# Two transformer blocks on one core: side work moved by some steps in the second block's projections

## The reference

```python
q, kv, gates, gq, gk, gv, glr, gout = split(rms_norm(h, attn_norm) @ w_in)
kc, vc, ks, vs, kw, vw = split(kv)              # 2 groups of 64 each
q = partial_rope(rms_norm(q, q_gain), pos) * scale
# compressed branch: windows of 32 tokens, stride 16, 31 of them
k_cmp = partial_rope(rms_norm(gelu((kc[blk] + pe_k) @ w1_k) @ w2_k, k_gains[0]), end)
v_cmp = gelu((vc[blk] + pe_v) @ w1_v) @ w2_v
o_cmp = masked_softmax(q @ k_cmp.T) @ v_cmp
# selected and window branches: keys ks and kw, normed and rotated, causal at 512 tokens
o_nsa = g0 * o_cmp + g1 * attend(q, ks, vs) + g2 * attend(q, kw, vw)
# gated linear attention, decays from glr
log_a = log_sigmoid(glr @ w_gate2 + b_gate) / 16
h = h + concat([o_nsa, gla(gq, gk, gv, log_a, gout)]) @ w_out
```

## Time and profile before

| | us |
|---|---|
| three runs | 1628.07, 1628.36, 1631.10 |
| median | 1628.36 |
| profiled execution, its own time | 1628.07 |
| its span | 1626.3 |

### The profile page before, as it was taken

One profiled execution on the slowest core, in us unless ns is written; L12 is line 12 of the kernel. 1 busy time (PEld: TensorE's weight loads), 2 busy tenths in 40 slices (PEclk: granted clock), 3 DMA queues, 4 the chain that ended last, 5 costly groups with the idle time before them and its releaser, 6 DMA issues.

```text
span 1626.3 us, 19784 instructions
## 1 busy us (share of the span) xinstructions
PE 1590.8 (98%) x8003; PEld 1268.0 (78%) x8003; DVE 881.5 (54%) x1628; ACT 614.2 (38%) x1069; POOL 43.8 (3%) x82
## 2 busy tenths in 40 slices
PE   6999999999999999999999999899999999999999
PEld 5877877678888888888888886666768888887887
DVE  6769785655375653232333655676457455555432
ACT  4443334542312432222322454466425334344320
POOL 1000000000000000000000101100000000000000
PEclk8999999999999999999999999999999999999999
DMA  7512121136245334322222151110113222222221
GB/s 299 198 65 103 53 75 69 53 129 246 104 168 168 104 131 155 104 91 101 86 99 99 34 188 47 39 53 14 40 53 116 91 104 91 88 85 100 104 78 52
DMA packets 44883, 165.76 MB, mean 102 GB/s; under 512 B 5108, under 2 KB 5236, under 8 KB 43640
## 3 DMA queue, kind: packets, MB, share of 16 engines
q1 hardware_dynamic: 44792, 164.50, 28.8%
HBM read 162.38 MB, written 2.10 MB: 101 GB/s over the span
## 4 chain that ended last, share of the span: by engine, by line
PE 91%; DVE 4%; ACT 2%; issue 1%; POOL 1%; DMA 0%; SPq 0%; DVEq 0%; ACTq 0%
PE bank L526 87%; PE bank L535 4%; DVE AR L1656 1%; DVE AR L1663 1%; DMA X<-in_x 0%; DVE wl L1644 0%; POOL ST L2420 0%; DVE X L1656 0%; ACT wh L1150 0%; ACT AR L1161 0%; ACT AR L1173 0%; DVE CST L1656 0%; POOL ST L2418 0%; DVE ST L1666 0%; DVE Hl L1656 0%
## 5 line engine op out<-in xcount | busy, mean ns | idle before, releaser
L526 PE MATMUL bank<-wh,Hh 128*128 128x512 f32 (+1 forms) x1008 | 408.8, 406 | 0.4 <-DVE wl L1644 0.4
L526 PE MATMUL bank<-wh,Hl 128*128 128x512 f32 (+1 forms) x1008 | 392.6, 390 | 0.0
L526 PE MATMUL bank<-wl,Hh 128*128 128x512 f32 (+1 forms) x1008 | 392.2, 389 | 0.0
L1150 ACT ACTIVATE wh<-raw 128x1024 fp32r<-128x1024 f32 (+2 forms) x195 | 203.6, 1047 | 403.6 <-PE bank L526 391.4
L1644 DVE TENSOR_TENSOR wl<-raw,wh 128x1024 fp32r<-128x1024 f32 (+2 forms) x195 | 234.3, 1209 | 138.9 <-ACT wh L1150 138.3
L526 PEld LDWEIGHTS bank<-wh,Hh 128*128 128x128 f32 x1008 | 190.5, 189 | 58.0 <-issue 21.7
L526 PEld LDWEIGHTS bank<-wh,Hl 128*128 128x128 f32 x1008 | 190.2, 189 | 40.5
L526 PEld LDWEIGHTS bank<-wl,Hh 128*128 128x128 f32 x1008 | 190.7, 189 | 34.3
L526 PE MATMUL bank<-Hh,wh 128*128 128x512 f32 (+2 forms) x504 | 190.5, 378 | 2.6 <-DVE AR L1663 1.2
L526 PE MATMUL bank<-Hh,wl 128*128 128x512 f32 (+2 forms) x504 | 189.4, 376 | 0.0
L526 PE MATMUL bank<-Hl,wh 128*128 128x512 f32 (+2 forms) x504 | 189.3, 376 | 0.0
(11 more groups left out here) (245 smaller groups left out, 1878.5 us busy)
## 6 DMA issues: line engine op xcount, KB each, us to landing
raw<-in_wst SPq DMA_DIRECT2D x268, 512.0 KB, 3.6
AR<-in_wst SPq DMA_DIRECT2D x8, 1024.0 KB, 6.5
X<-in_x SPq DMA_DIRECT2D x8, 512.0 KB, 4.9
AR<-in_wst SPq DMA_DIRECT2D x5, 512.0 KB, 6.0
out<-X SPq DMA_DIRECT2D x8, 256.0 KB, 2.1
CST<-in_cst SPq DMA_DIRECT2D x1, 1619.0 KB, 9.6
raw<-in_wst SPq DMA_DIRECT2D x4, 296.0 KB, 2.8
BC<-in_bc SPq DMA_DIRECT2D x2, 512.0 KB, 6.9
```

The costliest lines, as they stand in the source:

```text
L526: return e.matmul(o, l, r, start=start, stop=stop, skip_group_check=True)
L1150: e.activation(HI[slot[i]][:, 0:width(i)], raw[:, i % NR, 0:width(i)], ACT.Copy).then_inc(*w_hi.mark(i))
```

## The change

It moves side work between steps on TensorE, ScalarE and VectorE. No arithmetic changes. In terms of steps:

| work | before | now |
|---|---|---|
| `scale` of ks on VectorE | 2kw step 8 | 2kw step 4 |
| transposes and copies of ks | 2kw step 14 | 2kw step 12 |
| `comp` chunks 2 and 3 | 2nq steps 2 to 9 | 2nq steps 4 to 11 |
| transposes and copies of kw | 2nq step 9 | 2nq step 12 |
| first decay sum and its exponentials | 2nq step 12 | 2nq step 11 |
| gelu on ScalarE | 2nq step 10 | 2nq step 12 |
| gelu's transposes | 2nq step 11 | 2nq step 13 |
| `ck`, `cv` | 2nq step 13, bank 6 | 2nq step 14, banks 4 and 5 |
| transpose `kc` | 2gv step 2 | 2gv step 1 |
| first attention unit | 2gv step 2 | 2gv step 1 |
| `cscore` of the first query tile | 2gv step 4 | 2gv step 2 |
| from `cscore` to `pct` | 3 steps | 2 steps |
| from one `cscore` to the next | 4 steps | 3 steps |

The core of the diff (of several like edits one stands):

```diff
@@ TensorE
-                    w.after(15, lambda: turn_keys("ks"))
+                    w.after(13, lambda: turn_keys("ks"))
...
-                    w.after(10, lambda: turn_keys("kw"))
+                    w.after(13, lambda: turn_keys("kw"))
...
                         if q == 3:
                             x.then_inc(*small.mark(("comp", c)))
                         yield
+                    if c == 1:
+                        yield
+                        yield
...
                 yield
-                yield
                 on.wait_ge(*dve.of(("hid",)))
-                claim(6)
+                claim(4)
                 for k in (0, 1):
-                    x = mm(bank[6][0:64, 256:320], hid4[:, k, 0, :], ...
+                    x = mm(bank[4][0:64, 0:64], hid4[:, k, 0, :], ...
                 x.then_inc(*small.mark(("ck",)))
+                free[4] = dve.of(("ck", "read"))
+                claim(5)
...
-                            x = mm(bank[6][32 * r4:32 * r4 + 32, 64 * g:64 * g + 64], ...
+                            x = mm(bank[5][32 * r4:32 * r4 + 32, 64 * g:64 * g + 64], ...
                 x.then_inc(*small.mark(("cv",)))
-                free[6] = dve.of(("ck", "read"))
-                for _ in range(5):
-                    yield
+                free[5] = dve.of(("vc",))
+                yield
+                yield
+                yield
...
                     yield
                     yield
-                    yield
                     on.wait_ge(*dve.of(("cprob", i)))
...
             def second_attention():
-                yield
                 yield from attention(att2, ...
@@ ScalarE
-                w.after(15 if name == "ks" else 10, lambda: [out_(u) for u in (0, 1)])
+                w.after(13, lambda: [out_(u) for u in (0, 1)])
...
-                for _ in range(25):
+                for _ in range(27):
                     yield
                 on.wait_ge(*small.of(("comp", 3)))
                 e.activation(hidr, bank[7][:, 0:256], ACT.Gelu_apprx_tanh)...
@@ VectorE
-                w.after(9 if name == "ks" else 5, scale)
+                w.after(5, scale)
...
-                for _ in range(27):
+                for _ in range(28):
                     yield
                 on.wait_ge(*small.of(("hid",)))
```

More of the change, by code:

```diff
@@ L960, in compressed @@
                 yield
-                yield
                 on.wait_ge(*dve.of(("hid",)))
-                claim(6)
+                claim(4)
                 for k in (0, 1):
-                    x = mm(bank[6][0:64, 256:320], hid4[:, k, 0, :], W("w2k").rearrange("p (k d) -> p k d", k=2)[:, k, :], k == 0, k == 1)
+                    x = mm(bank[4][0:64, 0:64], hid4[:, k, 0, :], W("w2k").rearrange("p (k d) -> p k d", k=2)[:, k, :], k == 0, k == 1)
                 x.then_inc(*small.mark(("ck",)))
+                free[4] = dve.of(("ck", "read"))
+                claim(5)
                 for r4 in range(4):
@@ L969, in compressed @@
                         for k in (0, 1):
-                            x = mm(bank[6][32 * r4:32 * r4 + 32, 64 * g:64 * g + 64], hid4[:, k, 1, 32 * g:32 * g + 32],
+                            x = mm(bank[5][32 * r4:32 * r4 + 32, 64 * g:64 * g + 64], hid4[:, k, 1, 32 * g:32 * g + 32],
                                    W("w2v").rearrange("p (k d) -> p k d", k=2)[:, k, :], k == 0, k == 1)
                 x.then_inc(*small.mark(("cv",)))
-                free[6] = dve.of(("ck", "read"))
-                for _ in range(5):
-                    yield
+                free[5] = dve.of(("vc",))
+                yield
+                yield
+                yield
                 on.wait_ge(*dve.of(("ck", "two")))
@@ L1017, in decays @@
                     yield
-                for _ in range(3):
-                    yield
+                yield
+                yield
                 for t in range(T):
@@ L1488, in compressed @@
                 e.activation(hidr, bank[7][:, 0:256], ACT.Gelu_apprx_tanh).then_inc(*act.mark(("gelu",)))
-                for _ in range(11):
-                    yield
+                yield
+                yield
+                yield
+                yield
+                yield
+                yield
                 for i in range(T):
@@ L2182, in compressed @@
                     q4 = slice(32 * r4, 32 * r4 + 32)
-                    copy(vc[q4, :, r4, :], bank[6][q4, 0:P].rearrange("p (g d) -> p g d", g=2), *[("vc",)] * (r4 == 3))
+                    copy(vc[q4, :, r4, :], bank[5][q4, 0:P].rearrange("p (g d) -> p g d", g=2), *[("vc",)] * (r4 == 3))
                 n3 = TK[0:64, 0:64].rearrange("p (g d) -> p g d", g=1)
                 sq = TK[0:64, 128:192].rearrange("p (g d) -> p g d", g=1)
-                src, ss = bank[6][0:64, 256:320].rearrange("p (g d) -> p g d", g=1), ST[0:64, 60:61]
+                src, ss = bank[4][0:64, 0:64].rearrange("p (g d) -> p g d", g=1), ST[0:64, 60:61]
                 on.wait_ge(*small.of(("ck",)))
```

8 lines of the change are left out of this document (removed).

## The result

| | before | changed |
|---|---|---|
| runs | 4 | 4 |
| median, us | 1628.47 | 1640.52 |
| lowest to highest | 1628.07 to 1631.10 | 1638.69 to 1641.33 |
| span of the profiled execution | 1626.3 | 1638.6 |
| mean granted clock | 0.994 | 0.991 |

A forecast was written before the change was run, and what follows sets the result against it. TensorE, 98% busy, bounds the kernel through its pauses and clock. Pauses +4.3 and clock -0.6 gave +3.7 to +3.9; +3.9 was taken on 1628.07: 1632.0 us, 8-in-10 range 1627.0 to 1635.0.

The forecast's parts named there:

- about 10 us: TensorE's waits between 930 and 1250 us in the old trace, 0.6% of the span, bounding what removed pauses could win.
- A: Start of the compression matmuls, near 963: keys' scaling ahead of the last additions, a 4.5 us pause, 4.1 us more.
- B: Gelu, 1000 to 1018: the old wait of 3.05 goes, new waits sum to 3.65, so +0.6 us.
- C: Compressed keys and first scores, 1021 to 1038: waits of 4.35 against the old 4.25, +0.1 us.
- the three later ones: Three later TensorE waits of 0.3 to 0.4 us on VectorE's addition, one per further query tile, expected to stay.
- the fourth queries' scaling 2.25 and the probabilities stand together ahead of the transposes: 1.6: In C, TensorE waits 1.6 us for VectorE's scaling and probabilities (1.7) before the transposes, with 2.4 of TensorE work between.
- Clock: Low-clock term: -2.9 us for two old stretches, +1.5 at A, +0.8 for one stretch in B or C, together -0.6.
- Rival 3: Slower than forecast: the clock falls at A, in B and in C, +5.9 us, 1634.0; chance 0.12.
- Rival 1: Only A's cost is left, C's pause before the probabilities is covered, clock full behind A: 1628.7 to 1631.0; chance 0.28.
- rival 2: Faster: B and C lose their waits altogether and the low clock goes, against 5.6 at A: -4.6 us, 1623.5; chance 0.13.
- Rival 4: Each table switch on ScalarE also pays a drain, so B's two switches cost 2.8 us more: 1634.8; chance 0.03.
- The leading step taken out of the attention: Attention ends one step earlier, but the linear attention after it starts in the same step as before: gain nothing.

The follow-up runs named there:

- a_alone: The kernel before with only the keys' scaling after 5 steps instead of 9 and their turn after 13 instead of 15: 1634.76 us, ratio 1.0034.
- turn_early: The changed kernel with the turns and copies of the third and fourth queries' tiles one step earlier: 1636.30 us, ratio 1.0044 to the kernel before.
- fill_all: The changed kernel with idle matmuls, results not read, in six TensorE pauses and no wait removed: 1632.62 us, ratio 1.0022 to the kernel before.
- gelu_late: The kernel before with TensorE's transposes of the gelu's result two steps later and the decay sums one step later: 1625.17 us, ratio 0.9968.
- best: gelu_late with the gelu's transposes in bank 3 and the fourth queries' tile scaled one step later: 1618.84 us, ratio 0.9940 to the kernel before.
- combo: The changed kernel with undo_a, turn_early and bank6 together: 1628.99 us, ratio 0.9998 to the kernel before.
- undo_a: The changed kernel with the keys' scaling behind the last additions again and their turn after 15 steps: 1632.16 us, ratio 1.0021 to the kernel before.
- bank6: The changed kernel with ck and cv in bank 6 again instead of banks 4 and 5: 1634.75 us, ratio 1.0038 to the kernel before.
- fill: The changed kernel with idle matmuls in two pauses, before the compression and before the first probabilities' transposes: 1636.27 us, ratio 1.0036 to the kernel before.

## Why the prediction was wrong

- **What bounds the kernel**: right. Every edit changed the time through TensorE's pauses and clock, as the sum over twelve traces shows. The rows given for "about 10 us" add up to 8.9; the rest is a wait of 1.46 near 1220 that the change does not touch.
- **A**: right. Forecast a pause of 4.5 and 4.1 us more, measured 4.47 and 4.07; a_alone shows it by itself. The clock behind it was sized at 1.5 (bounds 0.6 and 3.1); 4.6 us of work at the low level are 0.46 x 4.6 = 2.1.
- **B**: the waits forecast were 0.35, 0.1, 1.6 and 1.6; measured are 0.34, 1.03, 1.69 and 1.58. The gelu's was missed. Two copies of the window keys, one of the queries and a weight tile stand ahead of its table load, which begins at 1010.84, while TensorE is there at 1011.55. The length of ScalarE's chain was right (5.25 forecast; 5.3 from 1009.23 to the end of the second decay's second exponential), but the sum left out the weight tile ahead of it (1008.28 to 1009.23). The decay sum's 1.69 hangs on the same chain: the two waits together are 2.72 against 1.7, so that 1.69 lies near 1.6 is partly luck. B came to 4.64 against 3.65.
- **C**: forecast 1.0, 0.75, 1.6 and, for the rest, 1.0; measured 1.15, 0.67, 3.62 and nothing, together 5.44 against 4.35. (The wait of 0.28 at 1049.73 is one of the three later ones, which stayed as forecast.) The step that failed is "the fourth queries' scaling 2.25 and the probabilities stand together ahead of the transposes: 1.6". It asks only when the operand is ready; that wait would have been 1.15, to the probabilities' end, so it was not too small. The bank that the transposes write was not looked at, and it came free 2.3 us later. turn_early took the sharing away and the pause went with it, though there the low clock ahead of the place had part in it. The trace of before already had such a wait: the third tile's turn, whose operand VectorE had finished by 1024.3, stood 1.77 us until VectorE had copied the compressed keys out of bank 2 (1030.12).

```profile
1030.40 0.66 PE L535 MATMUL bank<-CST,AR 128*128 128x128 f32 x4 [1.77 <-DVE PRMT L1669]
```

- **Clock**: the term "-2.9 for the two old stretches, +1.5 at A, +0.8 for one stretch in B or C", -0.6 in all, is the step of the sum that failed most. Measured: +6.6 us. The loss for each us of low work was right (0.47 forecast, 0.46 fitted). What was wrong is how much work fell under it: in B 3.4 us (1.6) and in C 13.3 us (6.1), where half a stretch had been put for both. Rival 3 had the right shape, the clock falls in A, B and C, but gave each place one stretch. That the stretches need the pauses, and that the small matmuls alone don't bring them, was shown by fill_all: full clock with all small matmuls in place and the pauses filled.
- **Sum**: pauses +6.8 against +4.3, clock +6.6 against -0.6. Of what the forecast lacked, 7.2 us are clock and 2.5 are pauses, of these 1.0 in B, 1.1 in C and the 0.5 that it took off for longer product steps, which no trace shows; 1.2 of it is missing in the span, since the first compression wait begins 1.2 us earlier in this execution than in that of before. The range ended at 1635.0 because it held one more stretch and no longer one.
- **Rival 1 and 2** (only A is left, or faster) are out: B and C together are 10.1 us of pauses, and 3 was the point below which rival 2 would have come. What they took for possible is real, though: gelu_late and best win at these same two places, with other moves.
- **Rival 4** (a drain at each table switch) is out. The table load at 1010.84 starts 0.02 after the copy before it ends, and the gelu 0.02 after the load, so there is no room for a drain. The Trainium skill (ScalarE: Activation LUTs, What ACT_TABLE_LOAD costs) adds a drain of some 1.4 us to each; neither kernel shows it.
- **The leading step taken out of the attention** was not tried by itself; in combo it stands and costs nothing that can be seen.

Not settled: why the clock stayed low through 13.3 us of nearly unbroken work behind the pause of 3.62, when it rose after 4.6 us of work behind the pause of 4.47 and after 3.4 behind B. Two traces show it alike, and with shorter pauses in C (undo_a, bank6) no such long stretch follows. Nor is it settled when the clock falls. With the same pauses of 1.58, 1.15 and 0.67 one after the other it fell within 1 us of the end of the last of them in undo_a, turn_early and fill, and in neither trace of the changed kernel. So the order of the work sets the pauses, but not by itself the low stretches, and how much of a single edit's gain is clock could not have been foretold from its pauses. What decides either, no run tells apart.

## What to carry to other kernels

When work is moved towards its reader, ask for each waiting instruction two times: when its operand is ready, and when the buffer that it writes is free; the second can hang on a third engine's queue. Where one engine is 98% busy, count its pauses twice, once as they stand and once for the clock: here each us of TensorE's work behind a standstill that runs at the low level costs 0.46 us more, and that came to as much as the pauses themselves. Here the cheap win was not to bring the producer forward but to let the waiting reader come later, behind product steps that were ready anyway.

## What the runs showed of the hardware

- Idle matmuls hold the clock: 53 of them in six pauses kept it at the full level for 99 us and took 7.9 us off the time. The Trainium skill (TensorE: Matmul & The Clock Gate, The HAM clock gate) says that "the default state is throttled, and activity releases the throttle". The runs agree in this: with the pauses filled the level stayed full, and behind A it rose after 4.6 us of work. Behind C it rose only after 13.3 us of work, which I had not expected.
- At the low clock a kernel's own waits get shorter (bank 2: 3.62 in the changed kernel, 2.18 in undo_a and 1.15 in bank6, all with the same order there). The other engines keep their speed: VectorE's 128x512 product takes 0.68 at 1039.43 in turn_early's low stretch and 0.69 at 1035.47 in the changed kernel at the full clock. A pause read from one trace is worth its length only while the clock ahead of it stays as it is.
- In the first 30 us of the program the low clock lasts 0, 7, 10 or 14 us in different executions, with no difference in the order there. It does not explain the spread of some 5 us between runs of one kernel: the profiled execution of before has 14 and took 1628.07, the fastest of its three, and that of fill_all has 7 and took 1631.09, where four runs with a granted clock of 1.00 took 1632.62 to 1633.07. best, in its five runs, spread by 0.5 us; what makes the others spread stays open.
